# A latent-attention head's queries in two pieces of 272 columns instead of 256, 256 and 32

## What is computed

```python
cq, ckv, kr = jnp.split(p, [Q_LORA, Q_LORA + KV_LORA], axis=-1)       # 256 | 128 | 32
q = jnp.einsum('bsc,chd->bshd', rmsnorm(cq, P['mla_q_norm']), P['mla_w_uq'])   # 8 heads x (64 + 32)
q_rope = apply_rope(q[..., QK_NOPE:], pos)
```

## Time and profile before

| | |
|---|---|
| runs | 2226.21, 2229.69, 2232.37 us; median 2229.69 |
| profiled execution | span 2231.6 us, from its first to its last instruction; of the three times, the nearest is 2232.37 |
| TensorE matmul | 2057.4 us busy, 92% |
| VectorE, ScalarE, GpSimd | 1137.8, 737.0 and 168.7 us busy |
| mean granted TensorE clock | 0.961 of full speed |
| the woven stage | about 158 to 464 us in the first layer, 1254 to 1563 us in the second |

### The profile page before, as it was taken

How to read it: one execution, slowest core, us unless ns; L and a number is a source line. 1 busy time by engine, 2 the same in 40 slices (tenths; PEclk the granted TensorE clock), 3 DMA queues, 4 the chain that set the end, 5 groups by cost and what they waited for, 6 DMA issues and landing times.

```text
span 2231.6 us, 34303 instructions
## 1 busy us (share of the span) xinstructions
PE 2057.4 (92%) x14674; PEld 1877.0 (84%) x14674; DVE 1137.8 (51%) x1911; ACT 737.0 (33%) x1392; POOL 168.7 (8%) x162
## 2 busy tenths in 40 slices
PE   6978999989979999999999799998998799999997
PEld 6947777779858999999998577776997599999997
DVE  6566666555333553444464766665543345444433
ACT  4253333355232421222323433334352332222212
POOL 2011111120001000000100111110100010000001
PEclk9989999989999999999999799999999999999998
DMA  5200000045302222222221000001361022222221
GB/s 202 80 7 1 1 1 1 6 165 167 108 19 66 77 87 93 86 85 95 85 86 48 7 1 1 1 1 42 115 208 48 19 76 88 93 86 89 84 93 60
DMA packets 38647, 149.54 MB, mean 67 GB/s; under 512 B 4384, under 2 KB 4544, under 8 KB 36832
## 3 DMA queue, kind: packets, MB, share of 16 engines
q1 hardware_dynamic: 36288, 130.89, 18.5%
q0 software_dynamic: 2208, 16.46, 1.9%
HBM read 139.65 MB, written 7.67 MB: 66 GB/s over the span
## 4 chain that ended last, share of the span: by engine, by line
PE 81%; DVE 12%; ACT 4%; issue 2%; POOL 0%; DMA 0%; DVEq 0%; SPq 0%; ACTq 0%; POOLq 0%
PE PS L438 79%; DVE stat L1510 1%; DVE X L1439 1%; PE PS L804 1%; DVE XT L1440 1%; DVE mP L1519 1%; PE PS L711 1%; DVE wL L1214 1%; ACT hH L835 1%; DVE MG L1429 1%; POOL sq L358 0%; DVE LG L1420 0%; ACT aP L835 0%; DVE stat L1511 0%; ACT L835 0%
## 5 line engine op out<-in xcount | busy, mean ns | idle before, releaser
L438 PE MATMUL PS<-hH,wH 128*128 128x272 f32 x2272 | 485.8, 296 | 30.8 <-DMA cst<-cst_in 15.4
L438 PE MATMUL PS<-hH,wL 128*128 128x272 f32 x2272 | 476.0, 291 | 0.0
L438 PE MATMUL PS<-hL,wH 128*128 128x272 f32 x2272 | 475.9, 291 | 0.0
L1214 DVE TENSOR_TENSOR wL<-ring,wH 128x1024 fp32r<-128x1024 f32 x238 | 301.0, 1266 | 221.1 <-ACT wH L835 220.6
L438 PEld LDWEIGHTS PS<-hH,wH 128*128 128x128 f32 x2272 | 360.2, 190 | 40.9 <-issue 17.7
L835 ACT ACTIVATE wH<-ring 128x1024 fp32r<-128x1024 f32 x238 | 249.8, 1051 | 357.3 <-PE PS L438 355.5
L438 PEld LDWEIGHTS PS<-hH,wL 128*128 128x128 f32 x2272 | 362.0, 190 | 0.0
L438 PEld LDWEIGHTS PS<-hL,wH 128*128 128x128 f32 x2272 | 360.1, 191 | 0.0
L438 PE MATMUL PS<-hidH,wL 128*128 128x272 f32 x1024 | 212.0, 288 | 0.0
L438 PE MATMUL PS<-hidH,wH 128*128 128x272 f32 x1024 | 211.7, 288 | 0.0
L438 PE MATMUL PS<-hidL,wH 128*128 128x272 f32 x1024 | 211.1, 288 | 0.0
(11 more groups left out here) (291 smaller groups left out, 2972.4 us busy)
## 6 DMA issues: line engine op xcount, KB each, us to landing
ring<-wall SPq DMA_DIRECT2D x238, 512.0 KB, 3.6
lw<-lw_in POOLq DMA_DIRECT2D x2, 2304.0 KB, 10.0
xT<-x_in SPq DMA_DIRECT2D x4, 544.0 KB, 6.0
y_out<-hT SPq DMA_DIRECT2D x8, 272.0 KB, 2.1
mem<-mem_in POOLq DMA_DIRECT2D x2, 1024.0 KB, 5.1
mks<-mks_in POOLq DMA_DIRECT2D x2, 1024.0 KB, 9.5
mvs<-mvs_in POOLq DMA_DIRECT2D x2, 1024.0 KB, 12.5
memk_out<-mkp POOLq DMA_DIRECT2D x2, 1024.0 KB, 5.6
```

The costliest lines, as they stand in the source:

```text
L438: return e.matmul(out, lhsT=a, rhs=b, start=start, stop=stop)
L1214: tt(wL[:, n % SPLIT], ring[:, n % RING], plain(wH[:, n % SPLIT]), ALU.subtract).then_inc(w_lo, 1)
```

## The change

PIECES has two entries of 272 columns. The count of pieces becomes NP = 2 and the number of projections of a head PROJ = NP + 2 = 4, in place of the literals 3 and 5. In the loop over units the projection of the next head is made behind units b = 0 to 3 and none behind b = 4: queries at b = 0 and 1, keys at b = 2 and 3. The attention starts with two projection steps instead of three. The list of bank uses gets nine entries a head, so scores and pieces change banks from head to head. Semaphore counts follow.

```diff
-PIECES = [(0, 256), (256, 512), (512, T)]
-USES = [("v", j) for j in range(5)] + [("p", 3), ("p", 4), ("v", 5), ("v", 6), ("p", 0), ("p", 1), ("p", 2)]
+PIECES = [(0, HALF), (HALF, T)]
+NP = len(PIECES)
+PROJ = NP + 2
+USES = [("v", j) for j in range(5)] + [("p", NP), ("p", NP + 1), ("v", 5), ("v", 6)] + [("p", _p) for _p in range(NP)]
 for _u, (_h, _b) in enumerate(UNITS):
     USES.append(("s", _u))
-    if _h + 1 < HEADS:
-        USES.append(("p", 5 * (_h + 1) + _b))
+    if _h + 1 < HEADS and _b < PROJ:
+        USES.append(("p", PROJ * (_h + 1) + _b))
...
 # TensorE, attention(); ScalarE and VectorE alike
-                    for p in range(3):
+                    for p in range(NP):
                         project(p)
                         yield
                     for u, (h, b) in enumerate(UNITS):
...
-                        if h + 1 < HEADS:
-                            project(5 * (h + 1) + b)
+                        if h + 1 < HEADS and b < PROJ:
+                            project(PROJ * (h + 1) + b)
...
-                        if h + 1 < HEADS and b < 3:
-                            queries_out(5 * (h + 1) + b)
+                        if h + 1 < HEADS and b < NP:
+                            queries_out(PROJ * (h + 1) + b)
                         normalise(u, "a", aP, *size(b))
```

More of the change, by code:

```diff
@@ L128 @@
     "lat_sq": 1, "lat_sum": 1, "lat_rstd": 1, "cq_n": 1, "ckv_n": 1, "kr_ready": 1,
-    "v_mm": 7, "v_out": 7, "q_mm": 3 * HEADS, "q_read": 3 * HEADS, "nope_out": 3 * HEADS, "q_out": 3 * HEADS, "k_mm": 2 * HEADS,
+    "v_mm": 7, "v_out": 7, "q_mm": NP * HEADS, "q_read": NP * HEADS, "nope_out": NP * HEADS, "q_out": NP * HEADS, "k_mm": 2 * HEADS,
     "k_out": 2 * HEADS,
@@ L300, in wait_bank @@
                 e.wait_ge(s["a_exp"], at(l, "a_exp", n + 1))
-            elif n % 5 < 3:
-                e.wait_ge(s["q_read"], at(l, "q_read", 3 * (n // 5) + n % 5 + 1))
-                e.wait_ge(s["nope_out"], at(l, "nope_out", 3 * (n // 5) + n % 5 + 1))
+            elif n % PROJ < NP:
+                e.wait_ge(s["q_read"], at(l, "q_read", NP * (n // PROJ) + n % PROJ + 1))
+                e.wait_ge(s["nope_out"], at(l, "nope_out", NP * (n // PROJ) + n % PROJ + 1))
             else:
-                e.wait_ge(s["k_out"], at(l, "k_out", 2 * (n // 5) + n % 5 - 2))
+                e.wait_ge(s["k_out"], at(l, "k_out", 2 * (n // PROJ) + n % PROJ - NP + 1))
         def in_turn(*programs):
@@ L667, in project @@
                 def project(n):
-                    h, p = n // 5, n % 5
+                    h, p = n // PROJ, n % PROJ
                     wait_bank(e, l, ("p", n))
                     o = bank(bank_of(("p", n)))
-                    if p < 3:
+                    if p < NP:
                         a, b = PIECES[p]
@@ L677, in project @@
                         last.then_inc(s["q_mm"], 1)
-                    elif p == 3:
+                    elif p == NP:
                         mm(o[0:64, :], W("uk", 64 * h, 64 * h + 64), ckv[:, 0:SEQ]).then_inc(s["k_mm"], 1)
@@ L687, in score @@
                     if b == 0:
-                        e.wait_ge(s["q_out"], at(l, "q_out", 3 * h + 3))
-                        e.wait_ge(s["nope_out"], at(l, "nope_out", 3 * h + 3))
+                        e.wait_ge(s["q_out"], at(l, "q_out", NP * h + NP))
+                        e.wait_ge(s["nope_out"], at(l, "nope_out", NP * h + NP))
                         e.wait_ge(s["k_out"], at(l, "k_out", 2 * h + 2))
@@ L1013, in nope_out @@
                 def nope_out(n):
-                    h, p = n // 5, n % 5
+                    h, p = n // PROJ, n % PROJ
                     if h >= 2:
                         e.wait_ge(s["a_score"], at(l, "a_score", 5 * (h - 1)))
-                    e.wait_ge(s["q_mm"], at(l, "q_mm", 3 * h + p + 1))
+                    e.wait_ge(s["q_mm"], at(l, "q_mm", NP * h + p + 1))
                     a, b = PIECES[p]
@@ L1024, in keys_out @@
                 def keys_out(n):
-                    h = n // 5
+                    h = n // PROJ
                     if h >= 2:
                         e.wait_ge(s["a_score"], at(l, "a_score", 5 * (h - 1)))
-                    e.wait_ge(s["k_mm"], at(l, "k_mm", 2 * h + n % 5 - 2))
-                    a, b = (0, SEQ) if n % 5 == 3 else (SEQ, KEYS)
+                    e.wait_ge(s["k_mm"], at(l, "k_mm", 2 * h + n % PROJ - NP + 1))
+                    a, b = (0, SEQ) if n % PROJ == NP else (SEQ, KEYS)
                     act(ak[0:64, h % 2, a:b], bank(bank_of(("p", n)), 0, b - a)[0:64, :],
@@ L1066, in attention @@
                         yield
-                        if h + 1 < HEADS:
-                            (nope_out if b < 3 else keys_out)(5 * (h + 1) + b)
+                        if h + 1 < HEADS and b < PROJ:
+                            (nope_out if b < NP else keys_out)(PROJ * (h + 1) + b)
                         if u:
@@ L1492, in queries_out @@
                 def queries_out(n):
-                    h, p = n // 5, n % 5
+                    h, p = n // PROJ, n % PROJ
                     if h >= 2:
                         e.wait_ge(s["a_score"], at(l, "a_score", 5 * (h - 1)))
-                    i = 3 * h + p + 1
+                    i = NP * h + p + 1
                     e.wait_ge(s["q_mm"], at(l, "q_mm", i))
```

## The result

| | before | after |
|---|---|---|
| median of 20 runs each | 2231.4 us | 2236.53 us |
| lowest to highest | 2224.29 to 2234.74 | 2231.8 to 2241.76 |
| ratio | | 1.0025, 95% interval 1.0016 to 1.0035 |
| profiled execution, span | 2231.6 | 2231.2 |
| the woven stage, both layers together | 611.5 | 611.7 |

The change makes the kernel slower, by 0.25%, 5 to 6 us: the interval lies wholly above 1, and the loss is smaller than the 0.3% that the prediction took as the least to tell from no change. The profiled execution of after (2233.03 us by its own time) is one of the quicker ones, so its span alone shows no loss; what it shows is where time went and where it came from. The woven stage, from the first scores to the first hL of the dense stage, takes 304.3 and 307.2 us before and 305.7 and 306.0 after.

What follows compares the result with a forecast made beforehand. TensorE was busy for 51.8 of 57.2 us of a first-layer group in the woven stage. Per layer 13.8 - 4 - 5 - 1.3 + 3 = +6.5, so +13 on 2229.7: 2242 us, range 2222 to 2257.

Steps and rivals of the forecast that it cites:

- (c): Opening of each group, scores to first X: 13.7 us against 14.7, so -1 an opening, -5 a layer (0 to -12).
- (f): New clock drops behind stalls: two of the six 1.7 us stalls, 1.5 us each, +3 a layer (0 to +9).
- slower by over 0.3%: Outcome above 2236.4 us, more than 0.3% or 6.7 us slower; given a chance of 0.58.
- The parity turns: Attention starts one step earlier in every group, so turn and score stand between P and X; sum +13 us.
- the removed work: One 32-column projection a head less on TensorE: costed at nothing, with 7.5 us as its far end.
- (b): Levels behind a rotation: the turn waits for VectorE's normalise, six stalls of 1.7 us and four of 0.9, +13.8 a layer.
- (a): Levels without a rotation: 5.8 us in all against 5.99, -4 us a layer over twenty levels.
- "faster" rival: The clock stops falling in the ten openings, 1.5 us each, -15; 2222 us; chance 0.17.
- openings that run at 2.4 GHz throughout: Sign in the changed profile that would show the forecast wrong: group openings keep the upper clock throughout.
- a granted clock at or under 0.95 in the groups: Sign for the forecast in the changed profile: the groups' granted clock is at or under 0.95.
- (e): The tail, last recurrence block to hH: 2.7 us instead of 4.0, -1.3 a layer.
- Rival "about the same": Normalise slips ahead of GpSimd's mask, each of twelve stalls 0.8 us shorter: +3, about 2230 us; chance 0.25.

Runs made afterwards that it cites:

- the one with the empty step: Changed kernel with one empty attention step behind the two first projections, so scores stand behind odd recurrence steps again: 2224.01 us, ratio 0.9963 against the kernel before.
- normalise-first kernel: Changed kernel with two lines exchanged on VectorE, the normalise ahead of the rotation: 2197.17 us, ratio 0.9853 against the kernel before; repeated, 2199.24 us, 0.9869.
- the second profile: Another profile of the changed kernel, span 2239.4 us; woven stage 308.8 and 312.9 us in the two layers.
- the waiting mask: Changed kernel where GpSimd alone waits, ahead of its masks of levels 2 to 4, for the normalise: 2210.94 us, ratio 0.9896 against the kernel before.
- new parity: Scores behind even recurrence steps, as in the changed kernel; given alone to the kernel before, with its three pieces: 2238.74 us, ratio 1.0036.
- old parity: Scores behind odd recurrence steps, as in the kernel before; with two pieces 2224.01 us, ratio 0.9963; with two pieces and normalise first 2215.93 us, 0.9933.

## Why the prediction was right or wrong

The forecast was 2242 us, slower, in a range of 2222 to 2257. Against the median that it started from, 2229.69, it added 13 us, 0.58%; measured are 0.25% (0.16% to 0.35%). The direction and the mechanism of the stalls hold, and the time, 2236.53 us, is in the range. The added time was put at more than twice the measured 5 to 6 us. That the time still fell near is in part luck, since two terms, (c) and (f), were each wrong by about as much as the whole sum, with opposite signs. The 0.58 for "slower by over 0.3%" was too sure: as a ratio it is 0.25%.

- *The parity turns, and that is what sets the time: right.* The prediction priced the parity at +13 and the removed work at nothing. Taken apart, the parity costs 14 us with two pieces (changed kernel against the one with the empty step) and 8 with three.
- *(b) The stalls: right*, and shown by three variants. Six places a layer were named; in the first layer the normalise takes 0.98 us or more at exactly six (178.7, 186.0, 249.8, 292.8, 354.8, 364.9), in the second at five. P to X there is 3.7 and 4.1 us where the clock holds, against 2.0 and 2.3 for the same units in the normalise-first kernel: 1.7 to 1.8, as forecast (1.7). At the four places of a layer without a mask TensorE waits 0.4 to 0.9 us, 2.7 together; the prediction took 0.9 each, 3.6.
- *(a) Levels without a rotation: right.* 3.5 + 2.1 to 2.7, so 5.6 to 6.2 us; the forecast mean was 5.8.
- *(c) The opening: the term that was furthest off.* The prediction took 1 us from each of ten openings, since it kept 1.5 us of low clock in it. In the profile of after none of the eight openings of groups 1 to 4 has a drop; they take 11.6 to 12.4 us, against 14.1 to 16.3 before, so 25 us went in eight openings instead of 8; in the second profile, where two of the eight have a drop, 22. Those of groups 0 keep their low clock and their length. Most of it is the mechanism of the "faster" rival, and the prediction's own sign against it (openings that run at 2.4 GHz throughout) came true in eight of ten; its other sign, a granted clock at or under 0.95 in the groups, in six of ten. The new stalls outweighed it, so "slower" stands. The rule on pauses that the prediction cites here from the Trainium skill's page "TensorE: Matmul & The Clock Gate", section "Why this matters for your kernels", is stated there for longer pauses than these of 1 to 2 us. In these traces such pauses were followed by a drop in some places and not in others.
- *(f) New drops: too small.* The changed kernel runs at half clock behind stalls in groups 0 and 3 of one layer and 0, 2 and 3 of the other. Of what the waiting mask brings back (29 us by the ratios, 20 in the profiles) 10 and 6 us are the waits themselves, so such drops cost 14 to 19 us and not the 6 of the sum. The errors of (c), 12 to 15 us too little gain, and of (f), 8 to 13 us too little loss, mostly cancel; what is left of the difference between 13 and 5 to 6 us is not placed by any run.
- *The removed work, costed at nothing: near enough in the changed kernel, wrong in the other orders.* In new parity three pieces and two are 1.0036 against 1.0025 and 1.0033, 1 to 2.5 us and inside the intervals. With the normalise first it is 0.2 to 0.35%, and in old parity 0.37%, 8 us. The profiles show where those 8 us lie, in the opening of group 3. The turn there, in the kernel before, then this opening in the kernel before and in the two-piece kernel of old parity:

```profile
339.33 0.55 PE L711 MATMUL PS<-cst,aP 128*128 128x128 f32 x3 [1.24 <-DVE aP L1519]
```

```profile
332.30:347.20 14.90, 12.89 (x65) 9.79 (x64) 9.35 (x17) 4.89 (x14) 3.04 (x2) 0.89 0.01 2
```

```profile
333.10:345.30 12.20, 11.37 (x65) 8.34 (x64) 8.68 (x14) 4.96 (x14) 2.99 (x2) 1.00 0.01 1
```

  The three short passes of the 32-column piece stand ahead of the normalise there. Without them TensorE does not wait for the turn, mv starts 0.7 us earlier and the clock stays up: 12.2 us in both layers instead of 14.8 and 16.3. That is 6.6 us, as much as the whole difference of the two profiles' stages (605.1 and 611.5). In new parity this opening takes 12.1 us with three pieces too. The prediction looked for the piece's worth on TensorE alone; it lies on VectorE and in the clock.
- *(e) The tail: right to a tenth.* VectorE is free for the last unit at 458.33, and hH starts 2.73 us later (4.0 before):

```profile
458.33 0.14 DVE L1519 RECIPROCAL stat<-stat 32x1 f32<-32x1 f32 x1
...
461.06 4.49 ACT L837 ACTIVATE hH<-hT 128x544 fp32r<-128x544 f32 x8
```

- *Rival "about the same" by a normalise ahead of the mask*: it happened at one place of twelve. At 1289.21, in the second layer and in a stretch at half clock, P ended late, the normalise started 0.08 us ahead of the mask and took 0.35 us, and TensorE waited 0.40. At the other eleven it starts behind the mask, by 0.27 us in the level shown.

## What to carry to other kernels

Where two programs are woven step by step, a step more or less at the start of one changes which operation stands ahead of which for the whole stage. Before removing a small piece of work, ask what it keeps in phase; here the piece was worth 8 us in the old phase and 1 to 2.5 in the new, and the change of phase cost 14. And once a removal changes the phase, read the new order for the one wait it creates: two lines exchanged on VectorE turned 0.25% slower into 1.4% faster. Put what another engine waits for first in every step, and what only has to be done by the next one behind it.

## What the runs showed of the hardware

- A VectorE normalise (a `tensor_scalar` from SBUF to SBUF) that starts while GpSimd multiplies two SBUF tensors ends only 0.1 to 0.3 us behind GpSimd's operation: 1.07 us instead of 0.29, again 0.29 when GpSimd is made to wait. An add of two SBUF operands does the same (1.44 instead of 0.43), and so does a copy in VectorE's side work (1.27 instead of 0.28 at 250.23 of the kernel before). VectorE's operations that read PSUM keep their time beside GpSimd: the first rotation pass takes 0.44 us with and without it. The normalise that starts first keeps its 0.29 us. That is what the Trainium skill's page "SBUF — State Buffer" says in "Who interferes with whom": a `tensor_scalar` in a two-port mode, or an operation with two SBUF inputs, and GpSimd exclude each other for the whole instruction.
- What such a wait costs is more than its length, through the clock: 12 collisions of 0.8 us were worth 29 us in all by the ratios, and 20 in the profiles, of which 14 were slower matmuls.
- Whether the clock falls in a pause is not set by the pause alone: the same opening with the same pauses ran at 0.50 in one kernel and at 1.00 in another, 15.4 and 12.4 us long. A single profile is therefore no measure for a change of this size; the medians of 4 to 20 runs are.
